# The last TensorE matmul ahead of a gate/up block, issued as two parts of 256 columns

## What is computed

```python
def swiglu(x, wg, wu, wd):          # x 256x1024, wg and wu 1024x2816, wd 2816x1024
    return (jax.nn.silu(x @ wg) * (x @ wu)) @ wd
...
for i in range(DEPTH):
    x = x + 0.5 * rmsnorm(swiglu(rmsnorm(x, g[0]), ...), g[1])
    x = x + rmsnorm(mixer(rmsnorm(x, g[2])), g[3])
    x = x + 0.5 * rmsnorm(swiglu(rmsnorm(x, g[4]), ...), g[5])
```

## Time and profile before

| | us |
|---|---|
| median of 3 runs | 2026.75 |
| lowest and highest | 2025.94, 2027.42 |
| the profiled execution | 2026.83 |
| its span, first to last instruction | 2024.4 |
| PE busy | 2005.5 |
| DVE busy | 1573.7 |
| ACT busy | 1093.8 |

### The profile page before, as it was taken

The page is one execution under the profiler, slowest core; times in us unless marked ns, Lnnn a source line. Parts: engine busy times, 40 slices in busy tenths (PEclk is TensorE's granted clock), DMA queues, the critical chain, the costliest instruction groups (busy, mean ns, idle before and its releaser), DMA issues.

```text
span 2024.4 us, 35859 instructions
## 1 busy us (share of the span) xinstructions
PE 2005.5 (99%) x14694; PEld 1864.8 (92%) x14694; DVE 1573.7 (78%) x1783; ACT 1093.8 (54%) x1208; POOL 26.6 (1%) x52
## 2 busy tenths in 40 slices
PE   9999999999999999999999999999999999999998
PEld 7999988998999999988998899998999899998998
DVE  7887678877887887768887987657887888677885
ACT  6545546555545665665555555645555555545553
POOL 0000000000000000000000000000000000000000
PEclk9999999999999999999999999999999999999999
DMA  6654745564555644435555555633555555654552
GB/s 260 227 208 181 250 151 192 198 226 152 207 206 187 223 174 159 155 126 187 203 192 208 187 196 222 226 136 135 205 192 207 187 198 201 225 194 152 200 195 104
DMA packets 56290, 386.36 MB, mean 191 GB/s; under 512 B 6752, under 2 KB 7136, under 8 KB 11232
## 3 DMA queue, kind: packets, MB, share of 16 engines
q1 hardware_dynamic: 52416, 372.07, 49.9%
q10 hardware_dynamic: 3744, 12.39, 1.8%
HBM read 383.39 MB, written 1.05 MB: 190 GB/s over the span
## 4 chain that ended last, share of the span: by engine, by line
PE 91%; DVE 6%; ACT 2%; issue 1%; DMA 1%; SPq 0%; POOL 0%; DVEq 0%; POOLq 0%; ACTq 0%
PE ps L551 22%; PE ps L553 22%; PE ps L552 22%; PE ps L557 6%; PE ps L559 6%; PE ps L558 6%; DVE w_low L1593 2%; PE ps L573 1%; PE ps L576 1%; PE ps L570 1%; PE ps L592 1%; DVE xn L1680 1%; DVE w_low L1698 1%; ACT w_high L1149 1%; ACT w_high L1224 1%
## 5 line engine op out<-in xcount | busy, mean ns | idle before, releaser
L1593 DVE TENSOR_TENSOR w_low<-raw,w_high 128x2048 fp32r<-128x2048 f32 x287 | 651.4, 2288 | 133.8 <-ACT w_high L1149 133.7
L551 PE MATMUL ps<-xT_both,w_high 128*128 128x256 f32 x2304 | 647.8, 281 | 0.0
L553 PE MATMUL ps<-xT_both,w_low 128*128 128x256 f32 x2304 | 647.2, 281 | 0.0
L552 PE MATMUL ps<-xT_both,w_high 128*128 128x256 f32 x2304 | 647.2, 281 | 0.0
L1149 ACT ACTIVATE w_high<-raw 128x2048 fp32r<-128x2048 f32 x287 | 546.5, 1911 | 44.2 <-DMA raw<-stream 34.6
L553 PEld LDWEIGHTS ps<-xT_both,w_low 128*128 128x128 f32 x2304 | 442.1, 192 | 0.0
L551 PEld LDWEIGHTS ps<-xT_both,w_high 128*128 128x128 f32 x2304 | 432.5, 188 | 4.4
L552 PEld LDWEIGHTS ps<-xT_both,w_high 128*128 128x128 f32 x2304 | 432.5, 188 | 4.4
L1193 ACT ACTIVATE region<-ps 128x256 f32<-128x256 f32 x176 | 67.3, 383 | 365.5 <-PE ps L553 356.9
L551 PE MATMUL ps<-w_high,oT_hi 128*128 128x512 f32 x576 | 226.3, 393 | 0.0
L553 PE MATMUL ps<-w_high,oT_lo 128*128 128x512 f32 x576 | 224.4, 390 | 0.0
(11 more groups left out here) (207 smaller groups left out, 2898.8 us busy)
## 6 DMA issues: line engine op xcount, KB each, us to landing
raw<-stream SPq DMA_DIRECT2D x351, 1024.0 KB, 4.8
gain<-gains ACTq DMA_DIRECT2D x23, 512.0 KB, 4.8
x<-x_in SPq DMA_DIRECT2D x2, 512.0 KB, 4.6
raw<-stream SPq DMA_DIRECT2D x2, 512.0 KB, 6.6
region<-rope_in SPq DMA_DIRECT2D x1, 512.0 KB, 5.7
out<-x SPq DMA_DIRECT2D x1, 512.0 KB, 2.7
att_mask<-att_mask_in SPq DMA_DIRECT2D x1, 320.0 KB, 6.1
out<-x SPq DMA_DIRECT2D x1, 256.0 KB, 2.1
```

The costliest lines, as they stand in the source:

```text
L551: nc.tensor.matmul(acc, lh, rh, start=start, stop=False, skip_group_check=goes_on)
L552: nc.tensor.matmul(acc, lh, rl, start=False, stop=False, skip_group_check=goes_on)
L553: return nc.tensor.matmul(acc, ll, rh, start=False, stop=stop, skip_group_check=goes_on)
L1593: nc.vector.tensor_tensor(w_low[:, p % RING, :], raw[:, p % RAW, :], w_high[:, p % RING, :], ALU.subtract).then_inc(piece_split, 1)
```

## The change

In each call of `seven` with c > 0, the last of its products is no longer issued by `products`. Its high·high and high·low matmuls stay at 512 columns, and the third, with `oT_lo` stationary, is issued as two matmuls of 256 columns into the two halves of the same bank. `seven(0)` is as before. The semaphore `piece_used` is raised by the second half, where it was raised by the whole.

```diff
@@ seven
+                        if c and bank == SEVEN[last - 1][0]:
+
+                            lh, ll = oT_hi_flat[:, tok], oT_lo_flat[:, tok]
+                            nc.tensor.matmul(ps[:, bank, :], lh, rh, start=False, stop=False)
+                            nc.tensor.matmul(ps[:, bank, :], lh, rl, start=False, stop=False)
+                            for part in range(2):
+                                some = slice(part * 256, part * 256 + 256)
+                                done = nc.tensor.matmul(ps[:, bank, some], ll, rh[:, some], start=False, stop=c == SEVENS - 1 and part == 1)
+                            continue
                         done = products(ps[:, bank, :], oT_hi_flat[:, tok], oT_lo_flat[:, tok], rh, rl, c == 0,
                                         c == SEVENS - 1)
```

## The result

| | before | after |
|---|---|---|
| median of 4 runs, us | 2027.09 | 2013.66 |
| lowest and highest | 2025.94, 2028.72 | 2012.79, 2015.55 |
| span of the profiled execution | 2024.4 | 2011.1 |
| PE busy | 2005.5 | 1986.5 |

The ratio is 0.9937, 95% interval 0.9925 to 0.9948: the change took 13.4 us by the medians, some 0.6%, off the kernel. The forecast, no change of cadence at 2027.7, was wrong. The case "all turn", to which it gave 0.32, is what happened to the blocks, but only half of its 25 us arrived.

What follows compares the result with a forecast made beforehand. PE's matmul cadence was taken to bound the kernel. The profiled 2026.83 us plus 0.93 for 104 splits gave 2027.8, set at 2027.7 because the profiled execution stood 0.08 above the median; range 2000.0 to 2029.5.

Steps and rivals of the forecast that it cites:

- What bounds the kernel: Whole kernel: PE's cadence sets the end, not waits; 256-column streams run steadily at 113.3 or 117.8 ns.
- Price of one place: Each of 104 split matmuls: two 256s for one 512 cost nothing to 8.9 ns; upper bound taken, 0.93 us.
- The waits at the places themselves: At the split places: waits stay; the block's wait, now behind 118 ns instead of 227, is still read ahead.
- No block changes its cadence: Blocks behind the halves stay at 117.8 ns; likeliest single case, 2027.7 us, chance 0.43.
- All change: Blocks 6 to 21 of eight FFNs fall to 113.3 ns: 25.9 us less 0.93, 2001.8 us, chance 0.32.
- I expect no new bound: If all blocks turn, PE needs 15.7 us in a unit where DVE is busy 13.68, leaving DVE 2 us.
- The 512s slow down: Unsplit 512s of the following `seven` lose 5.3 ns each, 6.6 us, with the split 7.5: 2034.3 us, chance 0.07.
- Half of it: Only blocks behind `w_high` places turn, 2011.4 us, or only those behind `corner` places, 2018.0 us; chance 0.18.

Runs made afterwards that it cites:

- `corner` places alone: Changed kernel with halves only where `corner` is the moving operand, six of thirteen places in an FFN: 2019.02 us, ratio 0.9961.
- `w_high` places alone: Changed kernel with halves only behind a whole `seven`, where `w_high` moves, seven of thirteen places in an FFN: 2019.85 us, ratio 0.9965.

## Why the prediction was wrong, point by point

**What bounds the kernel:** right. PE's cadence was the end, no wait, and the two cadences of 113.3 and 117.8 ns are what the 24.9 us of the blocks are made of.

**Price of one place:** taken at the upper bound of 8.9 ns, 0.93 us. The halves run at 113 and 119 ns, 24.18 - 23.58 = 0.6 us for all: between the bounds. The page of the Trainium skill that was weighed there, "TensorE: Matmul & The Clock Gate", "Back-to-back issue gap", would have 109.2 ns for either; neither half is that short. Its formula is given there for isolated matmuls, and this is a stream. The reason for taking the upper bound, that 256s directly behind 512s start at it, held for the second half and not for the first.

**The waits at the places themselves:** right. PE doesn't wait for the block's semaphores behind the halves: the first step of the block is 121 ns on the mean, without idle time.

**No block changes its cadence (0.43): this is the step that failed.** The prediction had the right rows, in the earlier trace rows: five of five places at which 256s with weights moving were followed by 256s with x moving turned to 113.3. It set against them that there were 24 to 84 narrow matmuls ahead there and only two here. The runs show that two are enough (98 to 104 of 104 places in six kernels that differ in place, stationary, order, width and number) and that one isn't. They also show that the reason given for the turn, a change of operand within 256s, was not the whole of it: with two 512s between the halves and the block it turned as well. The weighing held the absence of a rule against the rows; five of five should have carried more than no rule. The trace of before had a further hint, against the count above all: block 4, which the prediction used for its cadence alone, stands behind just two matmuls of 128 columns that follow 512s (in seven FFNs with a wait between), and four of the eight blocks 4 are short.

**All change (0.32): mechanism right, sum wrong.** The term of the blocks was right, 25.9 expected, 24.9 measured. What failed here is "I expect no new bound". It was drawn from DVE's mean share in one unit, 13.68 of 16.1 us, a stage in which that holds: none of the new wait of 5.9 us is there. The FFN's end, where blocks 18 to 21 follow each other and DVE has a 2.29 us piece in its order ahead of block 21's last steps, was not looked at. Over the kernel waits grew by 8.9 us with the restarts, 7.5 of it there; 7.4 us went away when only DVE's order of two steps was changed, and 7.5 us of the time (2013.66 to 2006.13).

**The 512s slow down (0.07):** as a whole it didn't happen, but there is a part of it in the result. The first three 512s behind a short block run at 232, 232 and 231 ns, then 227; with the rest this makes 1.6 us. With the halves too far ahead of the block it is all that is left, 3.5 us slower.

**Half of it (0.18):** its two prices were 2018.0 and 2011.4. The kernel with the `corner` places alone came to 2019.02, that with the `w_high` places alone to 2019.85, for the same reason as above: the first kind doesn't make PE early at the FFN's end, the second does.

**Open:** what in the hardware holds a stream at one cadence or the other. The experiments show only which entries lead where. What delays DVE's piece in the kernel with all three in halves is open too. For the single places that stay long (one to six of 104) the traces show the off step ahead of the halves and no experiment shows that it is the cause.

## What to carry to other kernels

When an engine is busy all the time, take the distance between starts for each kind of instruction and stage, not the busy time, and ask of any stream that has two of them what stands ahead of it, and at what step that was entered itself: here 0.6 us of narrower matmuls bought 24.9 us in the blocks, of which 13.4 us reached the time. When a bounding engine is made faster, look at the places where it waits least comfortably, not at the others' mean shares: list for each the last product that it needs, what stands ahead of that in its producer's order, and how many of the engine's own steps lie between. And try the two edits together: the order of DVE at the FFN's end was worth nothing alone and 7.5 us behind the other.

## What the runs showed of the hardware that was not expected

- The same stream of 256-column matmuls, each with its own weight load, runs at 117.8 ns when it is entered from 512s at 226.7, and at 113.3 when it is entered within some matmuls behind two parts of a 512 (256 + 256 in either order, 384 + 128, or two 256s with different stationaries). Two 512s between still turn it (102 of 104), five don't (0 of 104), a single 256 doesn't (0 of 104). It keeps its cadence for at least 192 matmuls.
- The way in takes some five longer steps: behind the halves of 113 and 119 ns the block goes 121, 122, 116, 114 and then 113.
- Behind halves, 512s take about 232 ns for at least five steps, and behind a block at 113.3 they take 231 to 233 for three and are then back at 227; behind a block at 117.8 in the kernel before they are at 227 from the first, but for three places of 112 (232 or 233).
- Where the 512 ahead of a pair of 256s takes 235 or 236 ns and the block stands right behind the pair, it stays at 117.8 (20 of 20 places).
- Behind idle times of 1.98 and 2.89 us, in the kernel with all three matmuls in halves, seven 512s in a row took 427 ns at a granted clock of 0.50.
- Narrow matmuls in a row with `oT` stationary run at 119 ns on the mean when there are six of them (624 in all), neither of the two cadences of the blocks.
